# Reciprocal row sums reach the queries' columns through one matmul a unit in place of two

## The chip, the cores and the metric

The kernel runs on one core of a Trainium2 chip. The metric is the device time of one execution in microseconds; the median of three runs of the kernel before is 3150.71 us (3149.67 to 3154.96).

## What is computed

One inference step of a hybrid layer, in fp32: a gated short convolution and a sparse attention run on the same input, are merged by gates and go through one output projection. The prompt has 2048 tokens, the decode batch 8 sequences of 8 tokens. What matters here is the prompt's attention: 8 query heads of 128 over 2 key-value heads, each query sees the 256 keys that an indexer picked.

```python
qg = q.reshape(b, t, N_KV_HEADS, N_HEADS // N_KV_HEADS, HEAD_DIM).astype(jnp.float32)
logits = jnp.einsum('btkgd,btnkd->btkgn', qg, k_sel) * (HEAD_DIM ** -0.5)
logits = jnp.where(valid[:, :, None, None, :], logits, NEG_INF)
p = jax.nn.softmax(logits, axis=-1)
o = jnp.einsum('btkgn,btnkd->btkgd', p, v_sel)
...
branch_b = attend(q, qi, wi, k, v, ki) * jax.nn.silu(z_b)
```

The kernel doesn't gather: it adds a mask of minus infinities to whole rows of logits. The softmax's division by the row's sum is the place of the change.

## The kernel before, in words

The prompt is cut into 4 tiles of 512 tokens. Each tile t does its input projections, then its attention (tiles 1 to 3 by `head_logits`, `head_values` and `lengths`; tile 0 by another routine that the change doesn't touch), then the output products. Each engine has its own program, written out in order, and semaphores join them; nothing reorders it.

The attention of a tile has 16 **units** (u = 0 to 15): 4 blocks of 128 queries times 4 pairs of heads. A unit of tile t and block b has n = 4t+b+1 blocks of 128 keys, taken two at a time in **groups** c = 0, 1, ...: 3 or 4 groups in tile 1, 5 or 6 in tile 2, 7 or 8 in tile 3. Matmuls run on fp32r operands (a rounded fp32), and precision is kept by splitting each operand in a high part, rounded to fp32r, and a low part, the rest. The steps of a unit, with the names of tiles that the rows show:

- PE, `head_logits(t, u + 1)`: the logits of the next unit, three matmuls (KHIGH, KLOW, QHIGH, QLOW) for each 512 keys. Just before the last piece of the second head it does `turn_p(t, u, 0)`: four transposes (L1339, `ps<-ident,LP`) that turn group 0 of this unit's exponentials.
- DVE, `mask_logits(t, u + 1)`: adds the mask (L2439, LP) and takes the row maxima (L2444). Between the two last pieces of the second head stands the first `probabilities_low`.
- ACT: the exponentials in place with their row sums into SUM (L1179), and `copy_p`, which writes the high part PTH of each turned group (L1192).
- DVE, `probabilities_low(t, u, c)` (L2422): the low part, PTL = turned probabilities less PTH.
- PE, `head_values(t, u)`: `turn_p(t, u, 1)`, then for each group c the transposes `turn_p` of group c + 2, the matmuls on PTL of group c - 1 (`low_values`, `ps<-PTL,VR`) and those on PTH of group c (`high_values`, `ps<-PTH,VR` and `ps<-PTH,VL`). The turned groups go round three PSUM banks, so that the transposes of group c + 3 wait until `probabilities_low` has read group c.
- DVE, `unit_sum(t, u)` (L2470 to L2473): the reciprocal of the two row sums, RIN, and its split. R4R holds four columns for each query: the high parts of both heads, then the low parts.
- POOL, `diagonals(t, u)` (L2792): DG = four 128x128 diagonal matrices, the identity times each column of R4R.
- PE, `lengths(t, u)`: ones times DG, which puts each query's reciprocal into its column of a PSUM bank, the same on all partitions. Two matmuls of 256 columns: the first on the high parts of both heads, the second adds the low parts. It stands behind `head_logits(t, u + 2)` and ahead of `head_values(t, u + 1)`; for the last unit it stands before the last group of its own `head_values`.
- DVE, `finish(t, u)` (L2463, TB; L2465, BB): the reciprocals times the gate, times the values.

DVE's order in a unit decides who waits:

```python
for c in range(1, groups if groups <= 4 else 3):
    probabilities_low(t, u, c)
    if c == 1 and u == len(UNITS) - 2:
        unit_sum(t, u)
if u < len(UNITS) - 2:
    unit_sum(t, u)
if u:
    finish(t, u - 1)
if groups > 4:
    probabilities_low(t, u, 3)
```

So in tile 1 the reciprocals come behind all groups of a unit, and in tiles 2 and 3 between group 2 and group 3. In unit 14 they stand behind group 1. `link` makes the next instruction of an engine wait for the one before it. POOL also writes the key cache KT (L2828, `whole_keys`) beside the units 13 and 14 of tiles 1 and 2. DMA and ACT have no part in the change.

Of the kernel before, what the change touches and what calls it, by code (L numbers as in the profile page):

```python
# [30 lines left out]
F32, F32R = mybir.dt.float32, mybir.dt.float32r  # L31
BF16, F16 = mybir.dt.bfloat16, mybir.dt.float16
U32, I32 = mybir.dt.uint32, mybir.dt.int32
ALU = mybir.AluOpType
# [3 lines left out]
P = 128  # L38
# [70 lines left out]
def program(nc, ins, outs, plan):  # L109
# [22 lines left out]
    def at(name, shape, dt, offset):  # L132
        return nc.alloc_sbuf_tensor_at(name, shape, dt, offset=offset)
# [5 lines left out]
    rKT, rV, rKH, rKL = region(16384), region(16384), region(8192), region(8192)  # L139
# [61 lines left out]
    ident = own("ident", [P, P])  # L201
    ones = own("ones", [P, P])
# [22 lines left out]
    RIN = small(84, 4).rearrange("p (u h) -> p u h", u=2)  # L225
# [93 lines left out]

    R4R = [at(f"R4R{i}", [P, 4], F32R, rJ + 4096 + 32 * i) for i in range(2)]  # L320
    R4 = [r[:, :].bitcast(F32) for r in R4R]
    DG = at("DG", [P, 4, P], F32R, rKH + 6144)
    TB = [at(f"TB{i}", [P, 256], F32, rKL + 6144 + 1024 * i) for i in range(2)]


# [14 lines left out]
    ps = [PS[:, i, :] for i in range(8)]  # L340
# [49 lines left out]
    def page_free(engine, n):  # L390
# [46 lines left out]
    qk, logits, row_max, expd, p_t, p_copy_a, pv, scaled, turned, attn_z = (  # L437
        signal(n) for n in ("qk", "logits", "row_max", "expd", "p_t", "p_copy_a", "pv", "scaled", "turned", "attn_z"))
# [3 lines left out]
    v_low, diag, p_low_dve = signal("v_low"), signal("diag"), signal("p_low_dve")  # L442
# [37 lines left out]
    UNITS = [(b, pr) for b in range(BLOCKS) for pr in range(HEADS // 2)]  # L480
# [834 lines left out]
    def _(pe):  # L1315
# [17 lines left out]
        def mm(out, lhsT, rhs, start=True, stop=True, **more):  # L1333
            return pe.matmul(out, lhsT, rhs, start=start, stop=stop, **more)  # L1334
# [9 lines left out]
        for k in range(KC):  # L1344
            ins_ = turn(ps[6][:, 16 * k:16 * k + 16], ST16[:, k * P:(k + 1) * P])
        ins_.then_inc(*prep_t.mark("state"))
        pe.wait_ge(*silu_c.at())
        for k in range(KC):
            ins_ = turn(ps[5][:, 9 * k:9 * k + 9], C9[:, k * P:(k + 1) * P])
# [445 lines left out]
        def lengths(t, u):  # L1795

            acc = acc_bank(t, u)
            pe.wait_ge(*diag.at(t, u))
            for part_ in range(2):
                ins_ = mm(ps[acc][:, 256:512], ones[:, :].bitcast(F32R), DG[:, 2 * part_:2 * part_ + 2, :].rearrange("p h q -> p (h q)"),  # L1800
                          part_ == 0 and u + 1 < len(UNITS), part_ == 1, skip_group_check=True)
            ins_.then_inc(*turned.mark(t, u))
            freed[acc] = attn_z.at(t, UNITS[u])

# [165 lines left out]
    def _(dve):  # L1970
        def link(ins_):

            ins_.then_inc(*dve_step.mark(dve_step.n))
            dve.wait_ge(dve_step.sem, dve_step.n)
# [493 lines left out]
        def unit_sum(t, u):  # L2468
            dve.wait_ge(*expd.at(t, u, 1))
            link(dve.reciprocal(RIN[:, u % 2, :], SUM[:, u % 2, :]))  # L2470
            if t:
                link(dve.tensor_copy(R4R[u % 2][:, 0:2], RIN[:, u % 2, :]))
                dve.tensor_tensor(R4[u % 2][:, 2:4], RIN[:, u % 2, :], R4[u % 2][:, 0:2], ALU.subtract).then_inc(*scaled.mark(t, u))  # L2473

        def attend(t):
            dve.wait_ge(*gate_mul.at(t, KC - 1, "P"))
# [159 lines left out]
    def _(pool):  # L2636
        def link(ins_):

            ins_.then_inc(*pool_step.mark(pool_step.n))
            pool.wait_ge(pool_step.sem, pool_step.n)  # L2640
# [147 lines left out]
        def diagonals(t, u):  # L2788
            pool.wait_ge(*scaled.at(t, u))
            if u:  # L2790
                pool.wait_ge(*turned.at(t, u - 1))
            pool.tensor_tensor(DG[:, :, :], ident[:, :].unsqueeze(1).to_broadcast([P, 4, P]),  # L2792
                               R4[u % 2].unsqueeze(2).to_broadcast([P, 4, P]), ALU.mult).then_inc(*diag.mark(t, u))

        def branch_low(f):
            if t and f == 2:
# [159 lines left out]
```

## Time and profile before

| | |
|---|---|
| median of 3 runs | 3150.71 us |
| the profiled execution: its own time | 3152.48 us |
| the profiled execution: its span | 3150.7 us |
| PE busy | 3095.8 us (98% of the span) |
| DVE busy | 1931.5 us (61%) |
| ACT busy | 1197.3 us (38%) |
| POOL busy | 896.8 us (28%) |
| TensorE clock granted, mean | 0.997 of full speed |

Spans and rows are those of the profiled execution, whose own time holds 1.8 us beyond the span. A busy share is a mean over the whole span; the three stretches in which the change lies are the attentions of tile 1 (about 1387 to 1495 us from the span's start), tile 2 (2078 to 2242 us) and tile 3 (2840 to 3060 us).

### The profile page before, as it was taken

To read this page: it belongs to the slowest core of one execution; us is meant where nothing else is said; L and a number is where in the kernel's file an instruction comes from. 1 tells how busy PE (TensorE), PEld (TensorE's weight loads), DVE (VectorE), ACT (ScalarE), POOL (GpSimd) and SP (SyncE) were. 2 spreads that over 40 slices of the span, in tenths; PEclk is the share of its full clock that TensorE was granted. 3 is DMA by queue.
4 is the path that set the end of the run, shared out by engine and by line. 5 is a ranking of instruction groups with operands and counts; after the bars stand their busy time and mean duration, and the time that the engine had idled before them with its cause. 6 is when DMAs were issued, how large, how long until landed. Compare 5 with 4: busy or idle time off the path is not lost.

```text
span 3150.7 us, 47465 instructions
## 1 busy us (share of the span) xinstructions
PE 3095.8 (98%) x18399; PEld 2694.2 (86%) x18399; DVE 1931.5 (61%) x3888; ACT 1197.3 (38%) x2092; POOL 896.8 (28%) x829
## 2 busy tenths in 40 slices
PE   7999999999999999999999999999999999999999
PEld 6999999966998888888888888889888788889997
DVE  5443597044434996039356999358537788878872
ACT  3444432345424221146235221155516444326550
POOL 2345675454520332013200331021310133111111
PEclk9999999999999999999999999999999999999999
DMA  8765688775874655640853656620573455660017
GB/s 299 258 209 196 211 277 285 283 255 184 287 257 160 182 200 205 226 157 23 292 199 132 212 188 210 231 86 15 198 245 120 161 195 193 215 229 26 10 62 257
DMA packets 271265, 600.89 MB, mean 191 GB/s; under 512 B 18973, under 2 KB 178903, under 8 KB 223938
## 3 DMA queue, kind: packets, MB, share of 16 engines
q1 hardware_dynamic: 260532, 559.96, 52.1%
q0 software_dynamic: 10368, 37.75, 3.5%
q8 instruction: 148, 2.42, 0.3%
q14 instruction: 75, 0.61, 0.1%
q10 hardware_dynamic: 142, 0.13, 0.0%
HBM read 455.22 MB, written 142.57 MB: 190 GB/s over the span
## 4 chain that ended last, share of the span: by engine, by line
PE 90%; DVE 4%; DMA 2%; issue 1%; ACT 1%; POOL 1%; SPq 0%; DVEq 0%; ACTq 0%; POOLq 0%
PE ps L1334 84%; PE ps L1339 6%; DVE PTL L2422 1%; DMA MW<-in_w_mod 1%; POOL WLH L2652 0%; DMA WLH<-w_scratch 0%; DVE LP L2439 0%; DVE SC L2199 0%; DMA WR<-in_w_proj_b 0%; DMA WR<-in_w_in 0%; ACT PTH L1192 0%; DVE OB L2450 0%; DVE RS L2155 0%; DMA GB<-gb_scratch 0%; DMA WR<-in_w_proj_a 0%
## 5 line engine op out<-in xcount | busy, mean ns | idle before, releaser
L1334 PE MATMUL ps<-HTH,WLH 128*128 128x512 f32 x3504 | 1129.9, 391 | 1.4 <-DMA WLH<-w_scratch 1.4
L1334 PEld LDWEIGHTS ps<-HTH,WLH 128*128 128x128 f32 x3504 | 657.8, 188 | 141.7 <-issue 5.8
L1334 PE MATMUL ps<-HTL,WLH 128*128 128x512 f32 x1752 | 682.1, 389 | 0.0
L2274 DVE TENSOR_SCALAR_CACHE_REDUCE JUNK<-SC,SMALL 128x1920 bf16<-128x1920 f32 (+5 forms) x364 | 514.3, 1413 | 16.9 <-POOL SC L2731 3.8
L1334 PE MATMUL ps<-H,WLH 128*128 128x288 f32 x3504 | 483.8, 298 | 6.5 <-POOL WLH L2652 2.3
L1334 PEld LDWEIGHTS ps<-H,WLH 128*128 128x128 f32 x3504 | 473.6, 190 | 9.0 <-POOL WLH L2652 3.0
L2439 DVE CUSTOM_DVE_ANT_0 LP<-ps,SC,RQ 128x512 f32<-128x512 f32 (+3 forms) x320 | 202.4, 666 | 299.8 <-PE ps L1334 299.1
L1334 PEld LDWEIGHTS ps<-HTL,WLH 128*128 128x128 f32 x1752 | 329.2, 188 | 65.6 <-issue 0.7
L1034 ACT ACTIVATE T<-ps 128x512 f32<-128x512 f32 x192 | 114.9, 599 | 649.2 <-PE ps L1334 637.9
L2652 POOL TENSOR_TENSOR WLH<-WR,WLH 128x1024 fp32r<-128x1024 f32 x97 | 234.7, 2420 | 314.7 <-ACT WLH L845 314.6
L2199 DVE SCALAR_TENSOR_TENSOR SC<-T,WI,SC 128x512 f32<-128x512 f32 (+3 forms) x266 | 180.1, 702 | 117.4 <-ACT T L968 116.8
L968 ACT ACTIVATE T<-ps 128x512 f32<-128x512 f32 (+3 forms) x304 | 162.5, 546 | 168.0 <-PE ps L1334 147.6
L1192 ACT ACTIVATE PTH<-ps 128x512 fp32r<-128x512 f32 (+1 forms) x264 | 146.9, 579 | 181.4 <-PE ps L1339 126.6
L845 ACT ACTIVATE WLH<-WR 128x1024 fp32r<-128x1024 f32 x97 | 102.9, 1061 | 242.6 <-DMA WR<-in_w_in 173.7
L2422 DVE TENSOR_TENSOR PTL<-ps,PTH 128x512 fp32r<-128x512 f32 (+1 forms) x264 | 167.0, 661 | 26.3 <-ACT PTH L1192 22.5
L1339 PE MATMUL ps<-ident,LP 128*128 128x128 f32 x1088 | 158.9, 274 | 0.9 <-DVE PTL L2422 0.5
L1179 ACT ACTIVATE LP<-LP,SMALL 128x128 f32<-128x128 f32 (+15 forms) x128 | 152.6, 1198 | 2.3 <-DVE SMALL L2444 2.3
L1339 PEld LDWEIGHTS ps<-ident,LP 128*128 128x128 f32 x1088 | 124.6, 140 | 19.6 <-issue 9.6
L1334 PE MATMUL ps<-PTH,VR 128*128 128x256 f32 x504 | 134.7, 288 | 0.7 <-ACT PTH L1192 0.7
L1334 PE MATMUL ps<-PTH,VL 128*128 128x256 f32 x504 | 130.3, 280 | 0.0
L2773 POOL CAST VR<-VO 128x512 fp32r<-128x512 f32 x6 | 3.7, 611 | 437.7 <-DVE VO L2128 437.7
L1334 PE MATMUL ps<-KHIGH,QHIGH 128*128 128x512 f32 (+3 forms) x320 | 123.2, 385 | 0.0
(372 smaller groups left out, 5145.2 us busy)
## 6 DMA issues: line engine op xcount, KB each, us to landing
WLH<-w_scratch SPq DMA_DIRECT2D x267, 1024.0 KB, 4.9
w_scratch<-WLH SPq DMA_DIRECT2D x97, 1024.0 KB, 5.5
WR<-in_w_in SPq DMA_DIRECT2D x73, 512.0 KB, 4.4
WLH<-w_scratch SPq DMA_DIRECT2D x48, 512.0 KB, 4.5
MW<-in_w_mod SPq DMA_DIRECT2D x6, 2048.0 KB, 16.4
q_scratch<-QO SPq DMA_DIRECT2D x32, 256.0 KB, 5.6
ma_scratch<-T SPq DMA_DIRECT2D x32, 256.0 KB, 5.6
gb_scratch<-GB SPq DMA_DIRECT2D x32, 256.0 KB, 5.9
```

The lines of the kernel that those rows point to most:

```text
L845: act.activation(WH[j % 3][:, :, :], WR[j % 3][:, :, :], ACT.Copy).then_inc(*w_high.mark(j))
L968: act.activation(T[1 + r % 4][:, 0:n], ps[bank("idx", t, b, h, c)][:, 0:n], ACT.Relu).then_inc(*relu.mark(r))
L1034: act.activation(paired(t, dst), src, func).then_inc(*evac.mark(j, p))
L1179: act.activation(row, row, ACT.Exp, bias=NM[:, u % 2, hh:hh + 1], accum_out=SUM[:, u % 2, hh:hh + 1]).then_inc(*expd.mark(t, u, hh))
L1192: act.activation((PTH if t else PT[t])[slot][:, 0:m], src, ACT.Copy).then_inc(*p_copy_a.mark(t, u, c))
L1334: return pe.matmul(out, lhsT, rhs, start=start, stop=stop, **more)
L1339: return pe.transpose(out, in_, ident[a:a + n, a:a + n])
L2199: dve.scalar_tensor_tensor(dst, x, w, dst, ALU.mult, ALU.add).then_inc(*scored.mark(r))
L2274: ins_ = dve.tensor_scalar(JUNK[0:n, 0:row.shape[1]], row, MID[0:n, c:c + 1], 0.0, ALU.is_ge, ALU.add, accum_out=CNT[0:n, c:c + 1])
L2422: dve.tensor_tensor(PTL[slot][:, 0:m], ps[bank("tr", t, u, c)][:, 0:m], PTH[slot][:, 0:m].bitcast(F32), ALU.subtract).then_inc(*p_low_dve. ...
L2439: ins_ = dve.tensor_tensor_reduce(LP[t][:, u % 2, hh, c:c + n], ps[bank("qk", t, u, hh, c)][:, 0:n], scores(t)[:, blk, c:c + n], RQ[:, blk ...
L2652: pool.tensor_tensor(WL[j % 3][:, :, :], WR[j % 3][:, :, :], WH[j % 3][:, :, :].bitcast(F32), ALU.subtract).then_inc(*w_split.mark(j))
```

## The change

R4R now holds, for each of the two heads, two columns e = 0 and 1. Query p of half e (partitions 0 to 63 are half 0, 64 to 127 half 1) has the high part of its reciprocal in row p, column e, and the low part in the row of the other half, p + 64 or p - 64, same column. DVE writes these with two copies and two subtractions on 64 partitions each, where it had one of each on 128; the low parts change partitions on their way out. TWICE is the sum of the left and right half of the identity: ones at (p, p mod 64). DG becomes TWICE times each of the four columns, 256 columns in place of 512: column (head, e, q) holds the high part in one half of the partitions and the low part in the other, and the ones add both up in one matmul. POOL makes TWICE anew once a tile, ahead of the first DG.

```diff
--- before.py
+++ after.py
@@ -319,7 +319,8 @@
 
     R4R = [at(f"R4R{i}", [P, 4], F32R, rJ + 4096 + 32 * i) for i in range(2)]
     R4 = [r[:, :].bitcast(F32) for r in R4R]
-    DG = at("DG", [P, 4, P], F32R, rKH + 6144)
+    DG = at("DG", [P, 4, P // 2], F32R, rKH + 6144)
+    TWICE = at("TWICE", [P, P // 2], F32, rKH + 7168)
     TB = [at(f"TB{i}", [P, 256], F32, rKL + 6144 + 1024 * i) for i in range(2)]
 
 
@@ -1796,9 +1797,8 @@
 
             acc = acc_bank(t, u)
             pe.wait_ge(*diag.at(t, u))
-            for part_ in range(2):
-                ins_ = mm(ps[acc][:, 256:512], ones[:, :].bitcast(F32R), DG[:, 2 * part_:2 * part_ + 2, :].rearrange("p h q -> p (h q)"),
-                          part_ == 0 and u + 1 < len(UNITS), part_ == 1, skip_group_check=True)
+            ins_ = mm(ps[acc][:, 256:512], ones[:, :].bitcast(F32R), DG[:, :, :].rearrange("p a q -> p (a q)"),
+                      u + 1 < len(UNITS), True, skip_group_check=True)
             ins_.then_inc(*turned.mark(t, u))
             freed[acc] = attn_z.at(t, UNITS[u])
 
@@ -2469,8 +2469,14 @@
             dve.wait_ge(*expd.at(t, u, 1))
             link(dve.reciprocal(RIN[:, u % 2, :], SUM[:, u % 2, :]))
             if t:
-                link(dve.tensor_copy(R4R[u % 2][:, 0:2], RIN[:, u % 2, :]))
-                dve.tensor_tensor(R4[u % 2][:, 2:4], RIN[:, u % 2, :], R4[u % 2][:, 0:2], ALU.subtract).then_inc(*scaled.mark(t, u))
+                ends = [slice(0, P // 2), slice(P // 2, P)]
+                high, both = (a.rearrange("p (h e) -> p h e", h=2) for a in (R4R[u % 2][:, :], R4[u % 2]))
+                for e, rows in enumerate(ends):
+                    ins_ = dve.tensor_copy(high[rows, :, e], RIN[rows, u % 2, :])
+                link(ins_)
+                for e, rows in enumerate(ends):
+                    ins_ = dve.tensor_tensor(both[ends[1 - e], :, e], RIN[rows, u % 2, :], both[rows, :, e], ALU.subtract)
+                ins_.then_inc(*scaled.mark(t, u))
 
         def attend(t):
             dve.wait_ge(*gate_mul.at(t, KC - 1, "P"))
@@ -2789,8 +2795,10 @@
             pool.wait_ge(*scaled.at(t, u))
             if u:
                 pool.wait_ge(*turned.at(t, u - 1))
-            pool.tensor_tensor(DG[:, :, :], ident[:, :].unsqueeze(1).to_broadcast([P, 4, P]),
-                               R4[u % 2].unsqueeze(2).to_broadcast([P, 4, P]), ALU.mult).then_inc(*diag.mark(t, u))
+            else:
+                link(pool.tensor_tensor(TWICE[:, :], ident[:, 0:P // 2], ident[:, P // 2:P], ALU.add))
+            pool.tensor_tensor(DG[:, :, :], TWICE[:, :].unsqueeze(1).to_broadcast([P, 4, P // 2]),
+                               R4[u % 2].unsqueeze(2).to_broadcast([P, 4, P // 2]), ALU.mult).then_inc(*diag.mark(t, u))
 
         def branch_low(f):
             if t and f == 2:
```

PE's order in tile 2: the end of `head_logits(2, 10)`, then `lengths(2, 8)`, then the transposes of `head_values(2, 9)`. Before:

```order
L1339 MATMUL ps<-ident,LP 128x128 x4
L1334 MATMUL ps<-KHIGH,QHIGH_111 128x384
L1334 MATMUL ps<-KLOW,QHIGH_111 128x384
L1334 MATMUL ps<-KHIGH,QLOW_109 128x384
L1334 MATMUL ps<-DG,ones 128x256 x2
L1339 MATMUL ps<-ident,LP 128x128 x8
L1334 MATMUL ps<-PTH_245,VR 128x256
```

Now:

```order
L1340 MATMUL ps<-ident,LP 128x128 x4
L1335 MATMUL ps<-KHIGH,QHIGH_111 128x384
L1335 MATMUL ps<-KLOW,QHIGH_111 128x384
L1335 MATMUL ps<-KHIGH,QLOW_109 128x384
L1335 MATMUL ps<-DG,ones 128x256
L1340 MATMUL ps<-ident,LP 128x128 x8
L1335 MATMUL ps<-PTH_245,VR 128x256
```

One matmul on DG is gone, behind the transposes of group 0 and ahead of those of groups 1 and 2; nothing else moved.

DVE's order in unit 5 of tile 2 (numbers behind a name tell buffers apart). Before:

```order
L2422 TENSOR_TENSOR PTL_249<-ps,PTH_246 128x512
L2422 TENSOR_TENSOR PTL_250<-ps,PTH_247 128x512
L2470 RECIPROCAL SMALL<-SMALL 128x2
L2472 CAST R4R_252<-SMALL 128x2
L2473 TENSOR_TENSOR R4R_252<-SMALL,R4R_252 128x2
L2463 TENSOR_TENSOR TB_254<-ps,SZB 128x256
L2465 TENSOR_TENSOR BB<-ps,TB_254 128x2x128
L2422 TENSOR_TENSOR PTL_248<-ps,PTH_245 128x512
```

Now:

```order
L2422 TENSOR_TENSOR PTL_249<-ps,PTH_246 128x512
L2422 TENSOR_TENSOR PTL_250<-ps,PTH_247 128x512
L2470 RECIPROCAL SMALL<-SMALL 128x2
L2475 CAST R4R_252<-SMALL 64x2 x2
L2478 TENSOR_TENSOR R4R_252<-SMALL,R4R_252 64x2 x2
L2463 TENSOR_TENSOR TB_255<-ps,SZB 128x256
L2465 TENSOR_TENSOR BB<-ps,TB_255 128x2x128
L2422 TENSOR_TENSOR PTL_248<-ps,PTH_245 128x512
```

Two instructions stand there in addition, ahead of `finish` and of the low part of group 3. Neither of the two waits for the instruction just before it: only the first copy and the first subtraction are linked.

## Rows read from the trace of the kernel before

**Rows 1.** Page: busy time of PE, and the chain that ended last, by line.
```profile
PE 3095.8 (98%) x18399; PEld 2694.2 (86%) x18399; DVE 1931.5 (61%) x3888; ACT 1197.3 (38%) x2092; POOL 896.8 (28%) x829
...
PE ps L1334 84%; PE ps L1339 6%; DVE PTL L2422 1%; DMA MW<-in_w_mod 1%; POOL WLH L2652 0%; DMA WLH<-w_scratch 0%; DVE LP L2439 0%; DVE SC L2199 0%; DMA WR<-in_w_proj_b 0%; DMA WR<-in_w_in 0%; ACT PTH L1192 0%; DVE OB L2450 0%; DVE RS L2155 0%; DMA GB<-gb_scratch 0%; DMA WR<-in_w_proj_a 0%
```
**Rows 2.** The tile DG: count, ns min/median/max, first and last start, forms.
```profile
L1334 PE MATMUL ps<-DG,ones x96: 276/280/336, 1397.9 to 3057.5; 128*128 128x256 f32 x96
L2792 POOL TENSOR_TENSOR DG<-ident,R4R x48: 1039/1040/1042, 1395.4 to 3049.0; 128x512 fp32r<-128x512 f32 x48
```
**Rows 3.** Timeline, PE, tile 2: start, duration, what, [idle before, releaser].
```profile
2202.57 0.40 PE L1334 MATMUL ps<-DG,ones 128*128 128x256 f32 x2
...
2202.80 1.04 PE L1339 MATMUL ps<-ident,LP 128*128 128x128 f32 x8
```
**Rows 4.** Timeline, tile 2, unit 1: DVE from the reciprocal on, PE's weight load.
```profile
2093.17 0.15 DVE L2470 RECIPROCAL SMALL<-SMALL 128x2 f32<-128x2 f32 x1
...
2093.36 0.17 DVE L2472 CAST R4R<-SMALL 128x2 fp32r<-128x2 f32 x1
...
2093.56 0.16 DVE L2473 TENSOR_TENSOR R4R<-SMALL,R4R 128x2 f32<-128x2 f32 x1
...
2093.64 0.42 DVE L2463 TENSOR_TENSOR TB<-ps,SZB 128x256 f32<-128x256 f32 x1
...
2094.10 0.42 DVE L2465 TENSOR_TENSOR BB<-ps,TB 128x256 f32<-128x256 f32 x1
...
2094.44 1.01 DVE L2422 TENSOR_TENSOR PTL<-ps,PTH 128x512 fp32r<-128x512 f32 x2
...
2095.18 0.30 PEld L1334 LDWEIGHTS ps<-PTL,VR 128*128 128x128 f32 x2 [0.43 <-DVE PTL L2422]
...
2096.88 0.75 DVE L2439 CUSTOM_DVE_ANT_0 LP<-ps,SC,RQ 128x512 f32<-128x512 f32 x1 [1.42 <-PE ps L1334]
```
**Rows 5.** Timeline, tile 2, units 7 and 8: PE's loads and DVE's group 3.
```profile
2154.45 0.30 PEld L1334 LDWEIGHTS ps<-PTL,VR 128*128 128x128 f32 x2 [0.32 <-DVE PTL L2422]
...
2163.89 1.61 DVE L2422 TENSOR_TENSOR PTL<-ps,PTH 128x512 fp32r<-128x512 f32 x3
...
2164.62 0.30 PEld L1334 LDWEIGHTS ps<-PTL,VR 128*128 128x128 f32 x2
```
**Rows 6.** Timeline, tile 3, units 2 and 6: group 3, transposes of group 6.
```profile
2875.45 2.57 DVE L2422 TENSOR_TENSOR PTL<-ps,PTH 128x512 fp32r<-128x512 f32 x4
...
2876.35 0.25 PEld L1339 LDWEIGHTS ps<-ident,LP 128*128 128x128 f32 x2
...
2927.81 1.99 DVE L2422 TENSOR_TENSOR PTL<-ps,PTH 128x512 fp32r<-128x512 f32 x3
...
2928.58 0.45 PEld L1339 LDWEIGHTS ps<-ident,LP 128*128 128x128 f32 x4
```
**Rows 7.** Timeline, tile 1, units 2, 8 and 13: DVE's groups and PE's loads.
```profile
1407.58 0.75 DVE L2439 CUSTOM_DVE_ANT_0 LP<-ps,SC,RQ 128x512 f32<-128x512 f32 x1 [0.19 <-PE ps L1334]
...
1441.60 1.28 DVE L2422 TENSOR_TENSOR PTL<-ps,PTH 128x512 fp32r<-128x512 f32 x2
...
1442.35 0.30 PEld L1334 LDWEIGHTS ps<-PTL,VR 128*128 128x128 f32 x2
...
1476.63 1.28 DVE L2422 TENSOR_TENSOR PTL<-ps,PTH 128x512 fp32r<-128x512 f32 x2
...
1477.65 0.31 PEld L1334 LDWEIGHTS ps<-PTL,VR 128*128 128x128 f32 x2
```
**Rows 8.** Timeline, tile 2, unit 14: DVE beside POOL's writes of KT.
```profile
2225.39 3.92 POOL L2828 TENSOR_TENSOR KT<-KLOW,KHIGH 128x384 f32<-128x384 f32 x4 [3.12 <-PE ps L1334]
...
2227.53 0.84 DVE L2472 CAST R4R<-SMALL 128x2 fp32r<-128x2 f32 x1
2228.40 0.93 DVE L2473 TENSOR_TENSOR R4R<-SMALL,R4R 128x2 f32<-128x2 f32 x1
2229.25 0.68 DVE L2422 TENSOR_TENSOR PTL<-ps,PTH 128x512 fp32r<-128x512 f32 x1
```

## The prediction

> **What bounds the kernel now.** I read the page first: PE is busy 98% of the span, and 90% of the chain that ended last lies on its two lines of matmuls and transposes [rows 1]. A matmul less on PE is therefore worth its time wherever PE really runs one instruction behind the other, and the page can't say where that is. So I went to the tile DG: 96 matmuls of 128x256, two for each of 48 units, and 48 products on POOL of 1.04 us [rows 2]. Their 280 ns are no price: they overlap. In the timeline the two start at 2202.57 and the transposes behind them at 2202.80 [rows 3], so both take 0.23 us of PE and one takes 0.117 us.
>
> The third view, the timeline of PE and DVE in the three attentions, decides. In tile 2, unit 1, PE's weight load for the low part of group 3 comes at 2095.18, after an idle time of 0.43 us that DVE ended [rows 4]. DVE's instruction had started at 2094.44 and takes 0.69, so the load follows its end by 0.05 us, the release. Back from there DVE is never idle: values, gate, subtraction, cast, reciprocal, groups 2 and 1, the maxima, group 0, and this one waits for ACT's copy of the transposes that PE did in `head_logits`. **Those transposes stand ahead of `lengths`, so the matmul that goes is not on this path, and the reciprocals that grow are.** PE waits so, with less and less idle time, up to 0.32 us in unit 7; in unit 8 the load at 2164.62 follows the low part (2163.89 + 0.69 = 2164.58) by 0.04 us, which is again the release with no slack [rows 5].
>
> **What goes and what comes.** PE: 48 x 0.117 = 5.6 us go, if PE runs without a wait behind each. That is the most the change can give.
>
> POOL: DG shrinks from 512 to 256 columns, from 1.04 to about 0.5 us. Three instructions for TWICE come, of 64 columns, each below that. PE reads DG only behind the logits of another unit, and no idle time of PE before its loads of DG is among the waits that I saw; that wait in the order covers both, so I cost them at nothing. Without the cover the half microsecond less on POOL would be a gain.
>
> DVE: one copy and one subtraction more a unit, each without a wait for the one before. No row has these on 64 partitions. The nearest: the subtraction starts at 2093.56 and lasts 0.16, but TB, which doesn't depend on it, starts at 2093.64, 0.08 us later; the dependent step from cast to subtraction takes 0.20 [rows 4]. So an unlinked small instruction costs the queue between 0.08 us (overlapped) and 0.17 (its whole duration). I take 0.08, since the new ones are exactly of the unlinked kind: **0.16 us a unit**; the upper end is 0.33. Below 0.08 I see no row; zero is the lower bound, if the halves of 64 were to run side by side.
>
> A rule of the Trainium skill speaks against this value. The page "VectorE: DVE Perf Modes", section on the TRN2 errata, puts the fixed term of a single instruction with operands in SBUF at about 150 cycles of 0.96 GHz, 0.156 us, and says that the latency is exposed between instructions; by it the two would cost 0.31 us a unit. The trace shows that duration (0.16 and 0.17) but starts the next independent instruction at half of it.
>
> **Unit by unit.** At the point where PE next waits for a low part, PE arrives 0.117 us earlier than before, and DVE 0.16 us later if the reciprocals lie ahead of that low part. With a slack s (load, less end of the low part, less 0.05 for the release) the unit changes by 0.16 - s there, by -s if the reciprocals lie behind, and by no less than -0.117.
>
> - Tile 1, the reciprocals behind all groups. In units 0 to 7 PE already stands at a low part: 0. In unit 8 group 1 ends at 1441.60 + 0.69 = 1442.29 and the load comes at 1442.35, so s is about 0.01; I read 0.01 to 0.08 in units 8 to 11: -0.2 together. In units 12 and 13 s is 0.28 (1477.65 less 1477.32, less 0.05): -0.117 each, -0.2 [rows 7]. What the longer reciprocals push is DVE's next mask; it waited 0.19 us for PE in unit 2, the tightest I noted, and takes up 0.16.
> - Tile 2, the reciprocals ahead of group 3. Units 0 to 11 have no slack: 12 x 0.15 = +1.8. Units 12 and 13 have about 0.15 and 0.11: +0.1.
> - Tile 3: here it is not a low part but the transposes of group 6 that come first, since they reuse the bank of group 3. In unit 2 group 3 ends at 2875.45 + 0.69 = 2876.14, the load comes at 2876.35: s = 0.16, change 0. In unit 6 it is 2928.50 and 2928.58: s = 0.03, change +0.1 [rows 6]. Read in the same way, units 1 to 3 give 0, 4 to 6 +0.3, 7 to 10 +0.2, 11 to 13 +0.1: +0.6, and unit 14, which waits for ACT behind `lengths`, -0.1.
> - Unit 14 of tiles 1 and 2: the reciprocals fall beside POOL's four or eight writes of KT, and PE waits for the low part behind them. In tile 2 cast and subtraction last 0.84 and 0.93 us, each to the end of one of POOL's instructions (0.98 apart, 2228.33 and 2229.31) [rows 8]. With two copies the second meets the second of these borders, and the subtractions find POOL done: about +0.3 in place of +0.15, in each tile: +0.6.
> - Unit 15: both its `lengths` come behind its own first transposes or between its values, where PE waits little. Tile 1 loses one of the two in a wait that follows: 5 x -0.117 = -0.6.
>
> The Trainium skill, "SBUF — State Buffer", section "Who interferes with whom", says that a cast, or an instruction with two inputs in SBUF, and a GpSimd instruction that reads SBUF lock each other out for a whole instruction. Where POOL is idle it changes nothing; here the trace agrees with it.
>
> **Sum:** -0.4 (tile 1) + 1.9 (tile 2) + 0.5 (tile 3) + 0.6 (units 14) - 0.6 (units 15) = +2.0 us. Against the profiled execution (3152.5 us) this is 3154.5; the median of the runs lies 1.8 lower, at 3150.7, and so I predict **3152.7 us**. About 0.2%, 6.3 us, is what a measurement of this kernel can tell from no change.
>
> **The rivals.**
>
> *A, PE keeps what it saves.* Every matmul counts, -5.6 us: 3145.1. For it: PE's 98% and the chain's 90% [rows 1]. Against it: the waits in rows 4 and 5. Even so it stays inside 0.2%.
>
> *B, the small instructions are free.* If the added two cost DVE next to nothing, the units that wait for DVE change by 0, and the others gain their slack or 0.117: tile 1 -0.5, tile 2 -0.2, tile 3 -1.2, units 15 -0.6, units 14 +0.2: -2.3, 3148.4. For it: rows that give a time of their own to two columns are few. Against it: 0.08 from start to start in rows 4.
>
> *C, the other side: DVE becomes the bound of tiles 2 and 3.* If an added instruction costs its full 0.17 us, the reciprocals push group 3 by 0.33. Tile 2 gives 12 x 0.32 + 2 x 0.2 = +4.2, tile 3 loses its slack everywhere: 14 units by 0.14 to 0.3, +2.9; with tile 1 at -0.4, units 14 at +0.8 and units 15 at -0.6 that is +6.9: 3157.6. It decides from about 0.3 us a unit on. For it: a release between the halves, or a penalty for the move across partitions, would do it. Against it: the start of TB. By the errata rule of the Trainium skill, page "VectorE: DVE Perf Modes", 0.31 us a unit, the sum would be about the same, +6.5.
>
> *D, the change doesn't do what it says*: PE could take the place of the removed matmul with a later start of the transposes, since these wait for banks of their own. Then PE gains nothing even in tile 1's units 12 and 13, which is +0.5 on the sum: 3153.2.
>
> **How the numbers follow.** The forecast 0.5, D 0.1, B 0.18, C 0.14, A 0.08. The range goes from 3147.9 to 3157.6: it takes in B and C whole and leaves out A. Faster by over 0.2% would take more than all 48 matmuls give: 0.03, for what I haven't seen. Slower by over 0.2% is most of C: 0.11. Within 0.2%: 0.86.
>
> **What would show it.** Right: 48 matmuls on DG; between the first copy's start and TB's in a unit of tile 2 about 0.44 us where there were 0.28 (2093.36 to 2093.64); PE's idle time before group 3's load in units 1 to 7 longer by about 0.28, and now a visible one in units 8 to 13; the period of a tile 2 unit longer by 0.15; in tile 3 an idle time of PE before the transposes of group 6. Wrong: DG's load preceded by a wait; the step to TB below 0.36 (B) or above 0.55 (C); tile 3's attention shorter by a microsecond or more (A or B).

## The result, and the profile after

| | before | after |
|---|---|---|
| median of 10 executions each, same chip, us | 3151.77 | 3161.56 |
| lowest to highest, us | 3149.67 to 3155.21 | 3159.89 to 3164.49 |
| profiled execution, us | 3152.5 | 3162.79 |
| its span, us | 3150.7 | 3161.0 |

The change makes the kernel slower: the ratio is 1.0031 (95% interval 1.0023 to 1.0039), which is 9.8 us. The forecast was 2.0 us more than before, with a range that ended at 3157.6.

Busy time and the chain that ended last, by engine, against [rows 1]. First the chain by engine of the kernel before, then both lines of the changed kernel:

```profile
PE 90%; DVE 4%; DMA 2%; issue 1%; ACT 1%; POOL 1%; SPq 0%; DVEq 0%; ACTq 0%; POOLq 0%
```

```profile
PE 3091.6 (98%) x18351; PEld 2686.0 (85%) x18351; DVE 1943.2 (61%) x3984; ACT 1196.2 (38%) x2092; POOL 879.2 (28%) x832
...
PE 87%; DVE 6%; DMA 2%; issue 2%; ACT 2%; POOL 1%; SPq 0%; ACTq 0%; DVEq 0%; POOLq 0%
```

The tile DG after, against [rows 2] (count, ns min/median/max, first and last start, forms):

```profile
L2800 POOL TENSOR_TENSOR DG<-TWICE,R4R x48: 612/613/617, 1395.7 to 3059.4; 128x256 fp32r<-128x256 f32 x48
...
L1335 PE MATMUL ps<-DG,ones x48: 280/282/337, 1397.5 to 3067.8; 128*128 128x256 f32 x48
```

So the matmul is gone and POOL's product is 0.43 us shorter, PE is 4.2 us less busy, and the whole span takes 10.3 us more. DVE's busy time grew by 11.7 us for 96 instructions more, and its share of the chain went from 4% to 6%. Tile 2, unit 1, of the timeline after shows how; these are the rows that answer to [rows 4] (start, duration, engine, line, what, [idle before, releaser]):

```profile
2094.28 0.15 DVE L2470 RECIPROCAL SMALL<-SMALL 128x2 f32<-128x2 f32 x1
2094.46 0.34 DVE L2475 CAST R4R<-SMALL 64x2 fp32r<-64x2 f32 x2
2094.84 0.32 DVE L2478 TENSOR_TENSOR R4R<-SMALL,R4R 64x2 f32<-64x2 f32 x2
2095.19 0.42 DVE L2463 TENSOR_TENSOR TB<-ps,SZB 128x256 f32<-128x256 f32 x1
...
2096.73 0.30 PEld L1335 LDWEIGHTS ps<-PTL,VR 128*128 128x128 f32 x2 [1.00 <-DVE PTL L2422]
...
2098.43 0.75 DVE L2439 CUSTOM_DVE_ANT_0 LP<-ps,SC,RQ 128x512 f32<-128x512 f32 x1 [1.43 <-PE ps L1335]
```

From the start of the cast to the start of TB there were 0.28 us; there are 0.73. The two casts take 0.34 us, the two subtractions 0.32: nothing overlaps. And TB, which started 0.08 us behind the start of the subtraction before, now starts behind the end of the second. Per instruction in the trace: copy to copy 0.175 us, subtraction to subtraction 0.167, second subtraction to TB 0.187. The two extra steps and the 0.108 that the third is longer are **0.45 us a unit** where the sum had 0.16. PE's idle time before group 3's load goes from 0.43 to 1.00 us: 0.45 for DVE, which is later, and 0.12 for PE, which is earlier. In this unit what the matmul saves is spent waiting.

PE's waits for a low part in tile 2's attention, before and then after (engine, tile, line, releaser: us in total, times, longest):

```profile
PEld ps L1334 <- DVE PTL L2422: 3.0, 8, 0.5
```

```profile
PEld ps L1335 <- DVE PTL L2422: 10.6, 15, 1.1
```

To see where the rest lies I take the starts of TB, one a unit, which no experiment below moves to another place among the groups. A period is the time from one to the next; a tile has 15, and since TB stands in the unit behind its own, the first is that of unit 2. From the first of tile 1 to the end of the program there are 1749.8 us before and 1760.1 after: all of the 10.3 us of the span. Tile 1's units give +0.6, tile 2's +5.4, tile 3's +3.0, and the two stretches between the attentions +0.9 and +0.4. What comes ahead of the first TB of tile 1, 1396 to 1407 us, is nearly all code that no kernel here changes, and it varies that much from one profiled execution to the next, so the table further down leaves it out.

### The profile page after: what moved, and what is told of

Read it like the earlier page. It is cut to its first block, busy times and chain, and to the rows that moved or that the text cites. A ratio compares the mean times of both kernels' runs of the same rounds, so it can differ in the third digit from the quotient of the medians.

```text
span 3161.0 us, 47468 instructions
## 1 busy us (share of the span) xinstructions
PE 3091.6 (98%) x18351; PEld 2686.0 (85%) x18351; DVE 1943.2 (61%) x3984; ACT 1196.2 (38%) x2092; POOL 879.2 (28%) x832
## 4 chain that ended last, share of the span: by engine, by line
PE 87%; DVE 6%; DMA 2%; issue 2%; ACT 2%; POOL 1%; SPq 0%; ACTq 0%; DVEq 0%; POOLq 0%
PE ps L1335 82%; PE ps L1340 5%; DVE PTL L2422 2%; DVE LP L2439 1%; ACT PTH L1193 1%; DVE TB L2463 0%; DMA WLH<-w_scratch 0%; POOL WLH L2658 0%; DVE BB L2465 0%; DMA WR<-in_w_proj_b 0%; DVE R4R L2475 0%; DVE SC L2199 0%; DMA ST<-in_state_conv 0%; DMA out_y_prompt<-YO 0%; DVE OB L2450 0%
## 5 line engine op out<-in xcount | busy, mean ns | idle before, releaser
L1335 PE MATMUL ps<-PTL,VR 128*128 128x256 f32 x504 | 115.8, 307 | 9.4 <-DVE PTL L2422 8.9
```

## The experiments

### Is it DVE, and the halves?

Four kernels on one chip, where the kernel before took 3150.72 us. The first has the halves on DVE but neither the single matmul nor the crossing of partitions:

```diff
-                link(dve.tensor_copy(R4R[u % 2][:, 0:2], RIN[:, u % 2, :]))
-                dve.tensor_tensor(R4[u % 2][:, 2:4], RIN[:, u % 2, :], R4[u % 2][:, 0:2], ALU.subtract)...
+                for rows in ends:
+                    ins_ = dve.tensor_copy(R4R[u % 2][rows, 0:2], RIN[rows, u % 2, :])
+                link(ins_)
+                for rows in ends:
+                    ins_ = dve.tensor_tensor(R4[u % 2][rows, 2:4], RIN[rows, u % 2, :], R4[u % 2][rows, 0:2], ALU.subtract)
```

> The kernel before with one edit: unit_sum's cast and subtraction are each written as two instructions, one for partitions 0 to 63 and one for 64 to 127, both in place; POOL's 1040 ns product and TensorE's two matmuls a unit stay. Theory T (it is the split into halves that costs: the second half, and the instruction behind, do not start before the one ahead has ended, as in the trace after, where cast to cast is 0.175 us, subtraction to subtraction 0.167 and subtraction to TB 0.187 against 0.079 before, together 0.45 us a unit, and DVE's time is on the loop of every unit of tiles 2 and 3): the same gaps here, and with no matmul saved a time above that of the change, 3162 to 3167 us. Rival R1 (what costs is that the low part is written into the other half of the partitions): subtraction to TB stays at 0.08 us and the second halves cost 0.08 each, 3154 to 3157 us. Rival R3 (the time comes from the new matmul, TWICE or POOL's product, not from DVE): 3151 to 3153 us.

Measured: 3162.51 us (ratio 1.0037, 1.0023 to 1.005). A unit of tile 2 in the timeline of DVE:

```profile
2155.75 0.34 DVE L2474 CAST R4R<-SMALL 64x2 fp32r<-64x2 f32 x2
2156.12 0.32 DVE L2477 TENSOR_TENSOR R4R<-SMALL,R4R 64x2 f32<-64x2 f32 x2
2156.48 0.42 DVE L2463 TENSOR_TENSOR TB<-ps,SZB 128x256 f32<-128x256 f32 x1
```

The same 0.73 us. R1 and R3 are out: nothing crosses here, and the new matmul and TWICE are absent. The whole loss is in how DVE's two instructions were cut.

The second takes the saving alone: DG and the one matmul take only the two columns of high parts, and the low parts are left out of the output.

> The kernel before with unit_sum untouched, and only the high parts spread: DG's product and the matmul take the first 256 columns, and the second matmul is gone. The low parts of the reciprocal sums are left out of the output. It is the saving of the change without its cost on DVE. Theory T: TensorE's 0.12 us a unit is swallowed in tile 2, where PE waits for PTL 0.43 us a unit anyway (0.74 after), and is worth up to 0.12 to 0.2 us a unit in tile 3 and at the end of tile 1, so 3148 to 3151 us. Rival R4 (the saving is on the path in every unit): 3145 to 3147 us. Rival R3 (the single matmul or the shorter product itself costs): 3153 us or more.

Measured: 3147.69 us, 3.0 less (0.9981 to 0.9999), 0.3 beyond the expected range. Tile 2 gets 0.5 us shorter, nearly all of it in its last four periods, and tile 3 2.15. So a matmul less is worth nothing where PE waits for DVE, and in tile 3 it is worth 0.14 us a unit on average, its full price of about 0.12 or a little more. The prediction's sum gave it next to nothing there; R4 would have given more than was measured.

The third adds as many instructions as the change, but on all partitions:

```diff
+                dve.tensor_copy(SPARE[0][:, 0:2], RIN[:, u % 2, :])
                 link(dve.tensor_copy(R4R[u % 2][:, 0:2], RIN[:, u % 2, :]))
+                dve.tensor_tensor(SPARE[1][:, 0:2], RIN[:, u % 2, :], R4[u % 2][:, 0:2], ALU.subtract)
                 dve.tensor_tensor(R4[u % 2][:, 2:4], RIN[:, u % 2, :], R4[u % 2][:, 0:2], ALU.subtract)...
```

> The kernel before with one more cast and one more subtraction in unit_sum, each on all 128 partitions and into a spare place, unlinked, ahead of the real one. As many DVE instructions as in the change, but none starts in another half of the partitions. Theory T: each starts some 0.08 us before the one ahead ends, so costs 0.08 us, 0.16 to 0.17 a unit, and TB still starts 0.08 us behind the subtraction: +4 to +5.5 us, 3155.5 to 3157.5 us. Rival R2 (any further small DVE instruction costs its full 0.17 us and more, whatever its partitions): the same as with the halves, 3162 us or more. Rival R5 (DVE's time is not on the path, only order is): within 1 us of before.

Measured: 3153.62 us, 2.9 more (1.0001 to 1.0019). DVE, a unit of tile 2:

```profile
2153.67 0.17 DVE L2473 COPY SPARE<-SMALL 128x2 f32<-128x2 f32 x1
2153.75 0.16 DVE L2474 CAST R4R<-SMALL 128x2 fp32r<-128x2 f32 x1
2153.94 0.16 DVE L2475 TENSOR_TENSOR SPARE<-SMALL,R4R 128x2 f32<-128x2 f32 x1
2154.02 0.16 DVE L2476 TENSOR_TENSOR R4R<-SMALL,R4R 128x2 f32<-128x2 f32 x1
2154.09 0.42 DVE L2464 TENSOR_TENSOR TB<-ps,SZB 128x256 f32<-128x256 f32 x1
```

Here is what I had forecast of the change: 0.08 us from an instruction's start to the next one's, and 0.42 from the first to TB, 0.14 more than before. R2 is out. The whole is 1.9 us below the range that I expected: tile 3 takes the 0.14 for nothing (-0.3 us), where I had counted it; tile 2 shows +1.4.

In the fourth DVE keeps only the reciprocal; POOL makes the four small steps of the change, each linked, ahead of its product.

```diff
             pool.wait_ge(*scaled.at(t, u))
+            for e, rows in enumerate(ends):
+                link(pool.tensor_copy(high[rows, :, e], RIN[rows, u % 2, :]))
+            for e, rows in enumerate(ends):
+                link(pool.tensor_tensor(both[ends[1 - e], :, e], RIN[rows, u % 2, :], both[rows, :, e], ALU.subtract))
```

> The changed kernel with the cast and the subtraction of each half moved to POOL, ahead of DG's product, each linked to the one before; DVE keeps the reciprocal alone. Theory T (DVE is on the loop of every unit in tiles 2 and 3): DVE gives back the 0.45 us a unit of the change and the 0.39 us of the old cast and subtraction, so 5 to 10 us under the kernel before, 3142 to 3147 us, and cast start to TB is gone (TB 0.08 us behind the reciprocal). Rival R6 (POOL's four linked instructions and the product make the turned matmul, and finish with it, late): 3150 us or more, with PE or DVE waiting for DG. Rival R2 as T here.

Measured: 3145.74 us, 5.0 under the kernel before (0.9971 to 0.9989). First DVE, then POOL, in one unit of tile 2:

```profile
2152.07 0.15 DVE L2470 RECIPROCAL SMALL<-SMALL 128x2 f32<-128x2 f32 x1
2152.14 0.40 DVE L2463 TENSOR_TENSOR TB<-ps,SZB 128x256 f32<-128x256 f32 x1
```

```profile
2152.29 0.42 POOL L2794 CAST R4R<-SMALL 64x2 fp32r<-64x2 f32 x2 [4.92 <-DVE SMALL L2470]
2152.79 0.46 POOL L2796 TENSOR_TENSOR R4R<-SMALL,R4R 64x2 f32<-64x2 f32 x2
2153.33 0.61 POOL L2801 TENSOR_TENSOR DG<-TWICE,R4R 128x256 fp32r<-128x256 f32 x1
```

POOL had been idle for 4.92 us, and in the whole program PE waits for DG once, for 1.0 us. PE's wait for PTL in tile 2, 3.0 us in the kernel before, is nearly gone:

```profile
PEld ps L1335 <- DVE PTL L2422: 0.7, 3, 0.2
```

### Why do two halves not overlap?

The kernel before, with groups of small unlinked copies added behind DVE's last work.

> The kernel before with some 45 unlinked small copies between spare columns appended at the end of DVE's work (its time is of no interest): groups of neighbours on all 128 partitions, on 0 to 63 alone, on 64 to 127 alone, on the halves in turn, on the four quarters, on 128 and a part in turn, and from one half into the other; some with 96 columns in place of 2. Theory T1 (an instruction waits out the one before whenever the two start at different partitions): 128 next to 128, 0-63 next to 0-63, and 64-127 next to 64-127 start 0.07 to 0.09 us before the end of the one before, and a change of the start 0.01 to 0.03 us after it. Rival T2 (any instruction that touches a partition from 64 up without 0 waits): 64-127 next to 64-127 also starts after the end. Rival T3 (any instruction of 64 partitions waits): 0-63 next to 0-63 also does. Rival T4 (it is the crossing between halves): only the groups that cross wait.

DVE's timeline in its one execution, one row for a group: start, time from the first start to the last end, form of the first, count. In order: all 128 partitions; 0 to 63; 64 to 127; 0 to 63 and 64 to 127 in turn; the four quarters; three copies from 0-63 into 64-127; from 0-63 into 64-127 and back in turn.

```profile
3154.58 0.38 DVE L2641 COPY PROBE<-PROBE 128x2 f32<-128x2 f32 x4
...
3154.99 0.37 DVE L2641 COPY PROBE<-PROBE 64x2 f32<-64x2 f32 x4
...
3155.39 0.38 DVE L2641 COPY PROBE<-PROBE 64x2 f32<-64x2 f32 x4
...
3155.81 0.69 DVE L2641 COPY PROBE<-PROBE 64x2 f32<-64x2 f32 x4
...
3156.54 0.68 DVE L2641 COPY PROBE<-PROBE 32x2 f32<-32x2 f32 x4
...
3158.63 0.30 DVE L2646 COPY PROBE<-PROBE 64x2 f32<-64x2 f32 x3
...
3159.31 0.69 DVE L2651 COPY PROBE<-PROBE 64x2 f32<-64x2 f32 x4
```

T1 holds. Four copies that start at the same partition take 0.37 to 0.38 us, whichever that is and however many partitions they span; four that change it take 0.68 to 0.69. Instruction by instruction, the next start comes 0.08 to 0.09 us ahead of the end where the start partition stays, and 0.013 us behind it where it changes. 128 partitions and then 0 to 63 overlap, 128 and then 64 to 127 don't: it isn't the number of partitions (T3), nor the upper half in itself (T2), and three copies in a row from the lower half into the upper overlap too, 0.30 us for the three (T4). Reads are compared with reads and writes with writes. One change costs 0.10 us.

The same can be seen in the trace of the kernel before, in the split of the index queries, whose writes are unlinked and alternate between the halves (DVE; L2144 writes partitions 0 to 63, L2145 64 to 127):

```profile
1597.92 0.18 DVE L2097 TENSOR_SCALAR WI<-ps 128x32 f32<-128x32 f32 x1
1598.02 0.42 DVE L2141 CAST T<-AS 128x512 fp32r<-128x512 f32 x1
1598.48 0.42 DVE L2144 CAST QI<-AS 64x512 fp32r<-64x512 f32 x1
1598.91 0.69 DVE L2145 TENSOR_TENSOR QI<-AS,T 64x512 fp32r<-64x512 f32 x1
1599.61 0.42 DVE L2144 CAST QI<-AS 64x512 fp32r<-64x512 f32 x1
```

The 128-partition cast starts 0.08 us ahead of the end of the row above it; 1598.48 + 0.42 = 1598.90, and L2145 starts at 1598.91; 1598.91 + 0.69 = 1599.60, and the next starts at 1599.61. The first L2144 and the L2145 behind it read the same partitions, so a change in what is written is enough; TB in the change is the other case, since it writes from partition 0 as the subtraction before it did, and only reads from another start. These rows have the pattern of the added instructions, and the prediction didn't read them.

Two doses of the same cost in the attention itself, on another chip, where the kernel before took 3152.04 us. First e3 with its spare instructions on partitions 64 to 127:

> e3 with its two spare instructions on partitions 64 to 127 in place of all 128: as many instructions, half the data. Theory T1 (an instruction that starts at another partition than the one ahead waits for its end, +0.014 us in place of -0.08): each spare one now costs 0.17 us and not 0.08, 0.35 us a unit against 0.16 in e3; tile 2 +4 us, tile 3 +0.2 us a unit for what is over its slack of 0.15, together 5.5 to 8.5 us above the kernel before. Rival R2 (only the number of instructions counts): as e3, +1.5 to +3 us.

Measured: 3158.49 us, 6.5 more than before (1.0015 to 1.0034), with half of e3's data. From the first copy (2152.11) to TB (2152.74) 0.63 us:

```profile
2152.11 0.17 DVE L2473 COPY SPARE<-SMALL 64x2 f32<-64x2 f32 x1
2152.29 0.17 DVE L2474 CAST R4R<-SMALL 128x2 fp32r<-128x2 f32 x1
2152.50 0.16 DVE L2475 TENSOR_TENSOR SPARE<-SMALL,R4R 64x2 f32<-64x2 f32 x1
2152.67 0.16 DVE L2476 TENSOR_TENSOR R4R<-SMALL,R4R 128x2 f32<-128x2 f32 x1
2152.74 0.42 DVE L2464 TENSOR_TENSOR TB<-ps,SZB 128x256 f32<-128x256 f32 x1
```

And the changed kernel with one change of partition fewer:

```diff
-                for e, rows in enumerate(ends):
-                    ins_ = dve.tensor_copy(high[rows, :, e], RIN[rows, u % 2, :])
-                link(ins_)
+                link(dve.tensor_copy(high, RIN[:, u % 2, :].unsqueeze(2).to_broadcast([P, 2, 2])))
```

> The changed kernel with the two casts of halves written as one on 128 partitions into all four columns, the two subtractions as they are: one change of the starting partition fewer. Theory T: 0.175 us a unit given back, 0.275 us left; tile 2 +3.5 us, tile 3 +1.7 us, tile 1 +0.3 us, together 4 to 7 us above the kernel before, half way back from the change. Rival R1 (the crossing subtractions are what costs): within 1 us of the change, +9 to +11.

Measured: 3155.31 us, 3.3 more than before (1.0005 to 1.0023), 0.7 below the range that I expected; R1 is out. From cast to TB there are 0.55 us, as T had it, and the stretch of the table below shows +4.1.

### Does the length count, or the place?

Three kernels. e7 is the change with `unit_sum` moved behind the last groups of `probabilities_low`, and e9 is the kernel before with the same move. In tile 1, where the sum already stood behind the groups, the moved call now stands behind `finish`, which the expectations don't mention. e5 is the kernel before with its cast and subtraction on POOL, which is e4 without the change.

```diff
-                if u < len(UNITS) - 2:
-                    unit_sum(t, u)
                 if u:
                     finish(t, u - 1)
...
                 for c in range(4, groups):
                     probabilities_low(t, u, c)
+                if u < len(UNITS) - 2:
+                    unit_sum(t, u)
```

> The changed kernel with one call moved: in tiles 2 and 3 unit_sum stands behind the last groups of probabilities_low instead of ahead of finish, where DVE waits 1.5 us a unit for the next scores anyway. All instructions of the change stay on DVE. Theory T (the cost of the change is its place ahead of the PTL that TensorE waits for, not its length): as e4 in tiles 2 and 3 (-0.4 us a unit and -0.13 against before), so 3143 to 3147 us. Rival R7 (DG comes 2 us later and the matmul, or finish, waits for it): 3150 us or more. Rival R10 (DVE's total time bounds the unit, wherever the sum stands): 3160 us.

> The kernel before with the same call moved, two matmuls a unit. Theory T: tile 2 gains some 0.4 us a unit and tile 3 nothing: 3146 to 3149 us, and e7 is 1 to 3 us faster, which is what the single matmul is worth once its instructions on DVE stand where they cost nothing. Rival R8 (the single matmul is worth nothing): the same time as e7. Rival R10: 3151 us.

> The kernel before with its cast and subtraction (128 partitions each, two linked instructions) moved to POOL, and its two matmuls and 1040 ns product kept: the second half of the move of e4 without the change. Theory T: tile 2 is bound by DVE, so it gives the same there as e4 (some 0.4 us a unit, 4 to 5 us) up to TensorE's own 0.12 us a unit, and nothing in tile 3, where e2 and e4 both gained only the matmul's 0.13 us a unit: 3146 to 3149 us, 1 to 3 us behind e4. Rival R8 (the single matmul is worth nothing by itself): the time of e4, 3145.7 us. Rival R9 (the single matmul is what made e4 fast): no faster than before.

On one chip, where the kernel before took 3152.91: e7 3146.67 (0.9975 to 0.9993), e9 3150.04 (0.998 to 0.9998), e5 3149.80 (0.9983 to 1.0001, so no certain gain in the medians). e7 is in its range. e9 and e5 end 1.0 and 0.8 us above theirs, but the kernel before took 2.2 us more on this chip than on the first four kernels'. DVE in e7, a unit of tile 2:

```profile
2148.89 0.15 DVE L2470 RECIPROCAL SMALL<-SMALL 128x2 f32<-128x2 f32 x1
2149.08 0.34 DVE L2475 CAST R4R<-SMALL 64x2 fp32r<-64x2 f32 x2
2149.45 0.32 DVE L2478 TENSOR_TENSOR R4R<-SMALL,R4R 64x2 f32<-64x2 f32 x2
2150.52 0.75 DVE L2439 CUSTOM_DVE_ANT_0 LP<-ps,SC,RQ 128x512 f32<-128x512 f32 x1 [0.74 <-PE ps L1335]
```

The wait for the same scores in the changed kernel:

```profile
2150.13 0.75 DVE L2439 CUSTOM_DVE_ANT_0 LP<-ps,SC,RQ 128x512 f32<-128x512 f32 x1 [1.54 <-PE ps L1335]
```

The whole sequence with its halves is still there. It lies in DVE's wait for the next scores, of which 0.74 us are left where there were 1.54. R7 and R10 are out: it was the place that made the length count. What the single matmul is worth in this place is less sure. The medians of e9 and e7 differ by 3.4 us, but each kernel's runs spread over 7 to 9 us; in the timelines tile 2 is 0.7 and tile 3 1.8 us shorter in e7, and tile 1 is 1.2 longer.

Last, two versions with the two casts written as one. e8 is e4 with it, e12 is e7 with it.

> e4 with POOL's cast written as one instruction on 128 partitions that fills all four columns (the two subtractions then overwrite the places of the low parts). POOL's chain ahead of DG's product gets some 0.2 us shorter. Theory T (after e4, TensorE bounds tiles 2 and 3, and POOL's chain is seen only at the ends of the attentions): within 1 us of e4 on the same chip, 4 to 7 us under the kernel before. Rival R6 (POOL's chain is on the path of every unit): 5 us faster than e4.

> e11 with unit_sum moved behind the last groups of probabilities_low in tiles 2 and 3, as in e7: all of the work on DVE, one cast. Theory T: in tiles 2 and 3 the sum's length no longer counts, so the time of e7 there, and tile 1, where the order is as before, gains some tenths: 6 to 7.5 us under the kernel before. Rival R10 (the length still counts behind the groups): more than 2 us faster than e7's -6.

Against 3152.04 on their chip: e8 3144.78 (0.9968 to 0.9987), e12 3145.79 (0.9971 to 0.9989). Both beat the kernel before and the changed one; between them and e4 or e7, which ran on other chips or at other times, the measurements don't decide. e8 is 0.3 us beyond its range of 4 to 7 us; whether it is within 1 us of e4 on one chip stays open, since it ran on another. e12 is in its range with -6.25, and R10 is out; but its expectation takes tile 1's order for unchanged, and there the call is moved as in e7.

### All of it in one table

"DVE": the time on DVE's queue between first cast and TB, against before, from the rows above; "none" and "moved" have no cast or subtraction there. Units: one period, always the sixth of tile 2 and the ninth of tile 3. Tile 2, tile 3: from the first to the last TB of the tile. Stretch: from the first TB of tile 1 to the end of the program in the profiled execution, against 1749.8. Median: against the kernel before on the same chip. All in us. What stands ahead of the first TB within its own unit lies outside the stretch, up to 0.5 us either way.

| kernel | DVE | matmuls | tile 2 unit | tile 3 unit | tile 2 | tile 3 | stretch | median |
|---|---|---|---|---|---|---|---|---|
| before | 0 | 2 | 10.22 | 14.09 | 147.4 | 196.7 | 1749.8 | |
| e3 full | +0.14 | 2 | 10.35 | 14.02 | 148.8 | 196.4 | +1.5 | +2.9 |
| e11 one cast | +0.27 | 1 | 10.48 | 14.24 | 150.7 | 197.5 | +4.1 | +3.3 |
| e10 upper half | +0.35 | 2 | 10.55 | 14.28 | 151.6 | 198.7 | +7.4 | +6.5 |
| e1 halves | +0.45 | 2 | 10.65 | 14.34 | 153.0 | 199.8 | +11.0 | +11.8 |
| **the change** | +0.45 | 1 | 10.65 | 14.41 | 152.8 | 199.7 | +10.3 | +9.8 |
| e2 high only | 0 | 1 | 10.22 | 13.92 | 146.9 | 194.6 | -3.8 | -3.0 |
| e5 on POOL | none | 2 | 9.81 | 14.10 | 144.2 | 197.3 | -3.4 | -3.1 |
| e4 on POOL | none | 1 | 9.78 | 13.92 | 143.1 | 195.3 | -6.2 | -5.0 |
| e8 on POOL, one cast | none | 1 | 9.82 | 14.00 | 143.2 | 195.5 | -7.0 | -7.3 |
| e9 sum last | moved | 2 | 9.81 | 14.04 | 144.1 | 197.0 | -3.7 | -2.9 |
| e7 sum last | moved | 1 | 9.72 | 13.98 | 143.4 | 195.2 | -4.9 | -6.2 |
| e12 both | moved | 1 | 9.72 | 13.99 | 143.7 | 195.1 | -5.8 | -6.3 |

A unit of tile 2 follows DVE one to one: +0.13, +0.26, +0.33, +0.43 for 0.14, 0.27, 0.35, 0.45, whether one matmul is there or two. A unit of tile 3 takes the first 0.15 for nothing and the rest in full: over its first twelve periods the means are 0.00, +0.12, +0.18 and +0.28 or +0.29. There the matmul counts only while DVE stays below 0.15.

## Why the prediction was wrong, step by step

- **The step that failed is the price of the two added instructions: "I take 0.08, since the new ones are exactly of the unlinked kind: 0.16 us a unit; the upper end is 0.33."** Being unlinked is one condition of the overlap, and the same start partition is the other. The change meets the first and breaks the second at three places: second copy, second subtraction, and TB, which isn't even edited. That is 0.16 + 3 x 0.10 = 0.46 us with the probe's price for each change, and 0.45 in the trace. The upper end took each added instruction at its full duration and left out that the one behind them could lose its own overlap, so the measured value lay outside the bounds as well. The row read for the price had only instructions on all 128 partitions; the rows at 1598 us had those that alternate. With 0.45 in place of 0.16 the prediction's own rules give +5.9 us in tile 2 and +4.3 in tile 3, and with its other terms as they stand about +9.8. That this is the measured value is in part luck: tile 3 cost only 3.0, while tile 1 and the stretches between the attentions grew by 1.9, for which the sum has nothing.
- The Trainium skill, "VectorE: DVE Perf Modes", section "Two Vector instructions with no wait between them", gives this as a model: a Vector instruction one of whose operands starts in another group of 32 partitions than the last read or write of that memory did is held until all earlier ones have finished. Trace and probe agree, TB among them (its SBUF input starts at 0, the subtraction before it read from 64); no run here has two different starts within one group of 32. The page names no price for being held; here it is 0.10 us. I weighed the errata section of the same page of the Trainium skill instead, and my estimate from it, 0.31 us for two instructions, fits neither case: e3's two cost 0.14, the change's 0.45.
- **Rival C was the right case**, at a chance of 0.14: DVE bounds tiles 2 and 3, by "a release between the halves, or a penalty for the move across partitions". e1 shows that the move isn't needed for the loss: halves in place cost as much. It is a wait between the halves, though no semaphore's. The prediction's own mark for C, over 0.55 us to TB, was met with 0.73. C's sum, +6.9, was short because its price, 0.33, was.
- *The path was right.* "The matmul that goes is not on this path, and the reciprocals that grow are": e2 gains 0.5 us in tile 2, the halves cost 5.6 there (e1). The step from price to time holds too: with 0.45 the prediction's rule gives +0.44 for a unit without slack, and the first eleven periods of tile 2 grew by 0.43 to 0.46; the twelfth grew by 0.25, where slacks of 0.15 and 0.11 would leave 0.30 to 0.34. The idle time before group 3's load was to grow by price plus matmul, and it did, by 0.57. What was said of DVE's cast beside POOL's writes of KT in unit 14 also held in tile 2: the two casts together took 1.80 us and ended with POOL's last write, and the subtractions found POOL done. Its size was short. From the reciprocal to the next low part 1.91 us became 2.38 in tile 2 and 0.95 became 1.50 in tile 1, +0.47 and +0.55 where +0.3 was forecast.
- *Tile 3 was read too tight.* I gave it slacks of 0.03 to 0.16 us and no saving. e3 costs it nothing, and its units behave as with one slack of about 0.15. e2 takes 2.15 us from it, so PE itself sets the pace there. The transposes of group 6 that came 0.03 us behind the release of group 3 [rows 6] can't have set the unit, or the period of unit 6 could have gained no more than 0.03 in e2; it gained 0.20. By the prediction's slacks 0.45 would have cost tile 3 some 4.4 us in its units 1 to 13; it cost 3.0 in all.
- *Tile 1* was to get shorter by 0.4 us, apart from its last two units, and got longer by 0.6 in all. Its early periods grew by up to 0.2, since 0.45 is more than the 0.19 us that DVE waited for PE [rows 7]; those of units 12 and 13 shrank by 0.15 and 0.12, about as forecast.
- *What was costed at nothing on POOL cost nothing.* PE never waits for DG in the changed kernel, and e1 without the shorter product and TWICE is as slow. The product takes 0.61 us where about 0.5 was estimated, which changes nothing.
- *The other rivals.* A's 5.6 us aren't all to be had even without the cost on DVE: e2 gained 3.0. B is excluded by e3, which costs tile 2 its 1.4 us, and D by e2.

The last periods of tile 1 are longer in e7 than in the change, the one that ends in unit 14 by 1.33 us, and its timeline tells why. About 0.92 us is only the place of the sum, which in e7 stands behind TB in unit 13 but ahead of it in unit 14, where the call wasn't moved. The other 0.4 us are real: in unit 14 the casts (0.86 us) and now also the subtractions (0.80 us) fall beside POOL's writes of KT.

What stays open: the first three periods of tile 2 take the same time in e4 and in e5, one matmul or two, and PE doesn't wait for PTL in them, so something else bounds them; the runs don't tell what. Nor do they tell why the stretches between the attentions grew by 0.9 and 0.4 us in the change.

## What to carry to other kernels

A small VectorE instruction that is cut into partition halves doesn't become two cheap ones: each change of the start partition costs the overlap with the neighbour, and the next, unedited instruction pays for the way back. Price an added instruction by rows of the same partition pattern, wherever in the program they stand. And where an engine waits once in every round, put work that grows into that wait, or on an idle engine, before counting what is saved elsewhere: the same change went from +9.8 us to -6.2 us, each against the kernel before on the same chip, by moving one call.

## What the runs showed of the hardware

- VectorE starts an instruction that isn't linked to the one ahead 0.08 to 0.09 us before that one ends when both read from the same start partition and both write to the same one, and 0.013 us after its end when either differs (0.03 for TB, which also reads PSUM): 0.38 against 0.69 us for four copies in e6. The number of partitions doesn't matter, nor that data moves between halves.
- A link between two small VectorE instructions costs more than an unlinked step: from the start of the cast to that of the subtraction 0.20 us, from there to the unlinked TB 0.08, in the kernel before.
- On GpSimd a copy of two columns on 64 partitions takes 0.21 us and a subtraction 0.23, with a link behind each (e4); a product of 256 columns takes 0.61 (the change) and one of 512 columns 1.04 (the kernel before).
